# Norm of the b projection done tile by tile within the second half of gated output a, with the split of its key/value weights

## The reference, cut to what matters

```python
            h = h + (o * jax.nn.silu(gate)) @ w_out_a[i]
        else:
            if layer == N_A_LAYERS:
                u_kv = rmsnorm(h, kv_norm_g)
                k_s, v_s = jnp.split(u_kv @ w_kv, [KV_WIDTH_B], axis=-1)
...
            u = rmsnorm(h, norm_b_g[j])
            q, gate = jnp.split(u @ w_in_b[j], [WIDTH_B], axis=-1)
```

## Time and profile before

| | |
|---|---|
| median of 3 runs | 2799.35 us (2794.68 to 2800.64) |
| the profiled execution: its own time | 2794.62 us |
| its span, first to last instruction | 2792.8 us |
| TensorE busy with matmuls | 2515.3 us, 90% |
| VectorE busy | 1630.2 us, 58% |
| ScalarE busy | 1351.0 us, 48% |
| mean granted TensorE clock | 0.965 |

### The profile page before, as it was taken

How to read it: one execution, slowest core, us unless ns; L and a number is a source line. 1 busy time by engine, 2 the same in 40 slices (tenths; PEclk the granted TensorE clock), 3 DMA queues, 4 the chain that set the end, 5 groups by cost and what they waited for, 6 DMA issues and landing times. The chain is left out here.

```text
span 2792.8 us, 38108 instructions
## 1 busy us (share of the span) xinstructions
PE 2515.3 (90%) x13535; PEld 1999.3 (72%) x13547; DVE 1630.2 (58%) x2854; ACT 1351.0 (48%) x2357; POOL 401.7 (14%) x558
## 2 busy tenths in 40 slices
PE   1899699999975999999977999997999897998989
PEld 1687369888754888888865878885666676886667
DVE  5663645587646999999957145412555517651751
ACT  3253144597335788888856132323555404322850
POOL 0122012230201211111111000001222200000330
PEclk9999899999997999999998999998999998999999
DMA  6542000000228999999967111033010212113301
GB/s 231 162 140 79 0 0 1 1 1 32 90 92 342 403 412 410 411 414 414 418 248 270 51 42 62 23 136 128 31 62 17 103 54 86 31 38 118 117 12 50
DMA packets 126957, 400.27 MB, mean 143 GB/s; under 512 B 11975, under 2 KB 62284, under 8 KB 114398
## 3 DMA queue, kind: packets, MB, share of 16 engines
q1 hardware_dynamic: 113754, 354.07, 33.4%
q0 software_dynamic: 12048, 42.56, 3.9%
q10 hardware_dynamic: 1012, 1.72, 0.2%
HBM read 347.93 MB, written 50.40 MB: 143 GB/s over the span
## 5 line engine op out<-in xcount | busy, mean ns | idle before, releaser
L2736 DVE CUSTOM_DVE_ANT_0 fox_l<-PS,fox_c 128x256 f32<-128x256 f32 (+7 forms) x128 | 92.1, 756 | 129.7 <-PE PS L2783 83.2
L2673 ACT ACTIVATE fox_l<-fox_l,stat 128x256 f32<-128x256 f32 (+7 forms) x128 | 98.3, 769 | 80.6 <-DVE stat L2736 80.5
L329 PE MATMUL PS<-wehg,xsTh 128*128 128x512 f32 x256 | 100.4, 392 | 8.3 <-DVE we0g_rest L2152 6.9
L329 PE MATMUL PS<-wehd,aTh 128*128 128x512 f32 x256 | 100.7, 393 | 6.6 <-DVE aTl L2171 6.6
L329 PE MATMUL PS<-wqkh,uTh 128*128 128x512 f32 x256 | 103.1, 403 | 0.0
L329 PE MATMUL PS<-wehu,xsTh 128*128 128x512 f32 x256 | 102.9, 402 | 0.0
L331 PE MATMUL PS<-wqkh,uTl 128*128 128x512 f32 x256 | 100.5, 392 | 0.0
L331 PE MATMUL PS<-wehd,aTl 128*128 128x512 f32 x256 | 100.4, 392 | 0.0
L331 PE MATMUL PS<-wehg,xsTl 128*128 128x512 f32 x256 | 100.2, 392 | 0.0
L331 PE MATMUL PS<-wehu,xsTl 128*128 128x512 f32 x256 | 100.1, 391 | 0.0
L330 PE MATMUL PS<-wqk_rest,uTh 128*128 128x512 f32 x256 | 100.0, 391 | 0.0
(11 more groups left out here) (579 smaller groups left out, 7525.4 us busy)
## 6 DMA issues: line engine op xcount, KB each, us to landing
we0g<-in_w_expert_gate SPq DMA_DIRECT2D x16, 2048.0 KB
we0u<-in_w_expert_up SPq DMA_DIRECT2D x16, 2048.0 KB
we1g<-in_w_expert_gate SPq DMA_DIRECT2D x16, 2048.0 KB, 11.2
we0d<-in_w_expert_down SPq DMA_DIRECT2D x16, 2048.0 KB
we1u<-in_w_expert_up SPq DMA_DIRECT2D x16, 2048.0 KB
we1d<-in_w_expert_down SPq DMA_DIRECT2D x16, 2048.0 KB
wada_rest<-in_w_ada SPq DMA_DIRECT2D x16, 1024.0 KB, 5.5
wada<-in_w_ada SPq DMA_DIRECT2D x4, 2048.0 KB, 12.9
```

What stands on the lines that cost most here:

```text
L329: nc.tensor.matmul(out, lh, rh, start=start, stop=False)
L2673: nc.scalar.activation(prob(p, e)[:, 0:K], prob(p, e)[:, 0:K], ACT.Exp, bias=nbm[:, u % 8:u % 8 + 1], scale=-1.0, accum_out=rsum[:, u % 16 ...
L2736: nc.vector.tensor_tensor_reduce(out=prob(p, e)[:, 0:K], in0=PS[:, 2 * e:2 * e + 2, :].rearrange("p a b -> p (a b)")[:, 0:K], in1=C[:, h % ...
```

## The change

A new function, `phase_gated_out_norm`, takes the place of gated output a and of the norm block. Its first half is as before. In the second half, when a token tile's right 512 columns have been added, the tile is complete, and its norm follows at once: ScalarE squares it and takes the root, VectorE scales it, and TensorE transposes it (8 blocks of 128x128) behind the next unit's matmuls. The key/value weights are loaded at the end of the first half and split in the second, with the gain as the scale of ScalarE's copy and of one VectorE operation, in eight pieces of 128x512. Output units use PSUM banks 0 to 3 (before 0 to 7), transposes banks 4 to 7. The b projection starts with its matmuls. Tiles move to other slots to make room.

```diff
+def phase_gated_out_norm(nc, A, env, sem, O, wo, loads, hi_slots, H, h_in, h_load, h_store, extra):
...
+    xn = [m.at(f"xn_nb{j}", 11, [P, D], kib=4 * j) for j in range(2)]
...
+    KV_AT = {1: (0,), 2: (1,), 3: (2,), 4: (3,), 5: (4,), 6: (5, 6), 7: (7,)}
...
+    def bank(t, half):
+        return PS[:, 4 + 2 * (t % 2) + half, :]
...
+            for u in range(2 * T):
+                n, t = u // T, u % T
+                sp.wait_ge(h_done, u + 1)
+                if u == T - 1:
+
+                    sp.dma_start(kv[:, :, :], chunk_of(A["w_kv_2"], slice(0, HALF))).then_inc(env.wkv_in, 16)
+                sp.dma_start(h_store[t * P:(t + 1) * P, n * HALF:(n + 1) * HALF], H[:, t, n * HALF:(n + 1) * HALF]
+                             ).then_inc(saved, 16)
...
+        @block.scalar
+        def _(act):
+            def high(t):
+                for half in range(2):
+                    act.wait_ge(t_ready, 2 * t + half + 1)
+                    nc.scalar.activation(turned(xTh, t, half), bank(t, half).rearrange("p (a b) -> p a b", b=P),
+                                         ACT.Identity).then_inc(x_hi, 1)
...
+            extra["act"](act)
+            act.wait_ge(o_mm, T)
+            for t in range(T):
+                act.wait_ge(h_done, T + t + 1)
+                if t >= 2:
+                    act.wait_ge(t_ready, 2 * (t - 1))
+                nc.scalar.activation(xn[t % 2][:, :], H[:, t, :], ACT.Square, accum_out=ss[:, t:t + 1]
+                                     ).then_inc(squares, 1)
+                act.wait_ge(squares, t + 1)
+                nc.scalar.activation(rs[:, t:t + 1], ss[:, t:t + 1], ACT.Sqrt, bias=env.eps[:, 0:1], scale=1.0 / D
+                                     ).then_inc(rms, 1)
+                if t:
+                    high(t - 1)
+                for k in KV_AT.get(t, ()):
+                    act.wait_ge(env.wkv_in, 16)
+                    nc.scalar.activation(kvh[:, k, :], kv[:, k, :], ACT.Identity, scale=gain[:, k:k + 1]
+                                         ).then_inc(kv_hi, 1)
+            high(T - 1)
...
+            for u in range(2 * T):
+                n, t = u // T, u % T
+                h = slice(n * HALF, (n + 1) * HALF)
+                dve.wait_ge(o_mm, u + 1)
+                nc.vector.tensor_tensor(H[:, t, h], PS[:, u % 4, :], H[:, t, h], ALU.add).then_inc(h_done, 1)
+                if n == 0:
+                    continue
+                for k in KV_AT.get(t - 1, ()):
+                    dve.wait_ge(kv_hi, k + 1)
+                    nc.vector.scalar_tensor_tensor(kvl[:, k, :], kv[:, k, :], gain[:, k:k + 1],
+                                                   kvh[:, k, :].bitcast(F32), ALU.mult, ALU.subtract)
+                one = slice(t, t + 1)
+                dve.wait_ge(rms, t + 1)
+                do(nc.vector.reciprocal(rs[:, one], rs[:, one]))
...
+                nc.vector.tensor_scalar(xn[t % 2][:, :], H[:, t, :], rs[:, one], None, ALU.mult).then_inc(xn_ready, 1)
+                if t:
+                    rest(t - 1)
+            for k in KV_AT[T - 1]:
...
+            rest(T - 1)
...
+            def turn(t):
+                pe.wait_ge(xn_ready, t + 1)
+                if t >= 2:
+                    pe.wait_ge(x_lo, 2 * (t - 1))
+                for half in range(2):
+                    for c in range(4):
+                        k = 4 * half + c
+                        last = nc.tensor.transpose(bank(t, half)[:, c * P:(c + 1) * P],
+                                                   xn[t % 2][:, k * P:(k + 1) * P], env.ident)
+                    last.then_inc(t_ready, 1)
...
+                if u >= 4:
+                    pe.wait_ge(h_done, u - 3)
...
+                if n == 1 and t >= 1:
+                    turn(t - 1)
+            turn(T - 1)
...
-            for p in range(4):
-                group_hi(0, p)
...
-            group_gain(0, 0)
-            for p in range(1, 4):
-                group_gain(0, p)
-                group_lo(0, p - 1)
-            group_lo(0, 3)
...
-    phase_gated_out(nc, A, env, sem, "a", env.O_a, env.wo_a, env.wo_a[1:], (8, 10), H, sem("h_in_a"),
-                    env.h_dram, [env.ha_dram], extra=trig)
-    env.wkv, env.wkv_in = m.at("wkv", 9, [P, KD, HALF]), sem("wkv_in")
+    env.wkv, env.wkv_in = m.at("wkv", 7, [P, KD, HALF]), sem("wkv_in")
+    env.wkvh, env.wkvl = m.at("wkvh", 8, [P, KD, HALF], F32R), m.rest("wkv")
     env.xT = (m.at("xTh", 3, [P, KD, S], F32R), m.at("xTl", 5, [P, KD, S], F32R))
-    phase_norm(nc, env, sem, "nb", H, None, [], 10, m.at("junk_nb", 7, [P, 2, D]),
-               prefetch=[(env.wkv, env.wkv_in, chunk_of(A["w_kv_2"], slice(0, HALF)))],
-               split=env.xT + (None,))
+    phase_gated_out_norm(nc, A, env, sem, env.O_a, env.wo_a, env.wo_a[1:], (8, 10), H, sem("h_in_a"),
+                         env.h_dram, env.ha_dram, trig)
     phase_b_projection(nc, A, env, sem)
```

More of the change, by code:

```diff
@@ L2883, in _, with wpiece, turned, do @@
                 last.then_inc(o_mm, 1)
+def phase_gated_out_norm(nc, A, env, sem, O, wo, loads, hi_slots, H, h_in, h_load, h_store, extra):
+    m, PS = env.m, env.PS
+    (Oh, Ol), (xTh, xTl) = O, env.xT
+    wl = [m.rest(f"wo_a{n}") for n in range(2)]
+    woh = [m.at(f"woh_a{n}", hi_slots[n], [P, KD, HALF], F32R) for n in range(2)]
+    xn = [m.at(f"xn_nb{j}", 11, [P, D], kib=4 * j) for j in range(2)]
+    kv, kvh, kvl = env.wkv, env.wkvh, env.wkvl
+    gain = env.cols[:, ROWS["kv_norm_g_2"]:ROWS["kv_norm_g_2"] + KD]
+    ss, rs, nw = env.stat[:, 0:T], env.stat[:, T:2 * T], env.stat[:, 2 * T:3 * T]
+    saved, w_hi, w_lo, o_mm, h_done = (sem("saved_a"), sem("w_hi_a"), sem("w_lo_a"), sem("o_mm_a"), sem("h_done_a"))
+    squares, rms, xn_ready, t_ready = sem("squares_nb"), sem("rms_nb"), sem("xn_nb"), sem("xnT_nb")
+    x_hi, x_lo, dve_step, kv_hi = sem("x_hi_nb"), sem("x_lo_nb"), sem("rstd_nb"), sem("kv_hi")
+    raw = [x[0] for x in wo]
+    KV_AT = {1: (0,), 2: (1,), 3: (2,), 4: (3,), 5: (4,), 6: (5, 6), 7: (7,)}
+    def wpiece(x, j):
+        return x[j // 4][:, 2 * (j % 4):2 * (j % 4) + 2, :]
+    def turned(x, t, half):
+        return x[:, 4 * half:4 * half + 4, t * P:(t + 1) * P]
+    def bank(t, half):
+        return PS[:, 4 + 2 * (t % 2) + half, :]
+    with nc.Block() as block:
+        @block.sync
+        def _(sp):
+            load(sp, loads)
+            for t in range(T):
+                sp.dma_start(H[:, t, :], h_load[t * P:(t + 1) * P, :]).then_inc(h_in, 16)
+            for u in range(2 * T):
[5 more added lines that the diff above has]
+                             ).then_inc(saved, 16)
+            sp.wait_ge(saved, 16 * 2 * T)
+        @block.gpsimd
+        def _(pool):
+            extra["pool"](pool)
+        @block.scalar
[5 more added lines that the diff above has]
+                                         ACT.Identity).then_inc(x_hi, 1)
+            for j in range(8):
+                act.wait_ge(wo[j // 4][1], 16)
+                nc.scalar.copy(wpiece(woh, j), wpiece(raw, j)).then_inc(w_hi, 1)
+            extra["act"](act)
+            act.wait_ge(o_mm, T)
+            for t in range(T):
+                act.wait_ge(h_done, T + t + 1)
[13 more added lines that the diff above has]
+            high(T - 1)
+        @block.vector
+        def _(dve):
+            step = Steps(dve_step)
+            def do(instruction):
+                dve.wait_ge(dve_step, step.mark(instruction))
+            def rest(t):
+                for half in range(2):
+                    dve.wait_ge(x_hi, 2 * t + half + 1)
+                    nc.vector.tensor_tensor(turned(xTl, t, half), bank(t, half).rearrange("p (a b) -> p a b", b=P),
+                                            turned(xTh, t, half).bitcast(F32), ALU.subtract).then_inc(x_lo, 1)
+            for j in range(8):
+                dve.wait_ge(w_hi, j + 1)
+                nc.vector.tensor_tensor(wpiece(wl, j), wpiece(raw, j), wpiece(woh, j).bitcast(F32), ALU.subtract
+                                        ).then_inc(w_lo, 1)
+            extra["dve"](dve)
+            dve.wait_ge(h_in, 16 * T)
+            for u in range(2 * T):
[12 more added lines that the diff above has]
+                do(nc.vector.reciprocal(rs[:, one], rs[:, one]))
+                do(nc.vector.tensor_tensor(nw[:, one], rs[:, one], rs[:, one], ALU.mult))
+                do(nc.vector.scalar_tensor_tensor(nw[:, one], ss[:, one], EPS * D, nw[:, one], ALU.add, ALU.mult))
+                do(nc.vector.tensor_scalar(nw[:, one], nw[:, one], -0.5 / D, 1.5, ALU.mult, ALU.add))
+                do(nc.vector.tensor_tensor(rs[:, one], rs[:, one], nw[:, one], ALU.mult))
+                nc.vector.tensor_scalar(xn[t % 2][:, :], H[:, t, :], rs[:, one], None, ALU.mult).then_inc(xn_ready, 1)
+                if t:
+                    rest(t - 1)
+            for k in KV_AT[T - 1]:
+                dve.wait_ge(kv_hi, k + 1)
+                nc.vector.scalar_tensor_tensor(kvl[:, k, :], kv[:, k, :], gain[:, k:k + 1],
```

(29 more changed lines are left out.)

23 lines of the change are left out of this document (11 added, 12 removed).

## The result

The changed kernel takes **2774.86 us** (median of 4 runs, 2770.27 to 2776.55) against 2798.80 us before (4 runs, 2794.68 to 2800.64): ratio 0.9916 (below 1 is faster), 95% interval 0.9905 to 0.9928. The forecast was 2775.8 us. One execution of an experiment, the one with one more square per tile, took 5166 us, for no reason that is known; it is left out of that experiment's median. The profiled execution took 2770.27 us with a span of 2768.1, 24.7 less than the 2792.8 of the earlier trace rows.

The account below looks back on a forecast made before the run. TensorE, busy 90% of the span, bounds the kernel, so only its idle or slow stretches can pay. 27.5 - 5.6 - 0.1 + 0.6 = 22.4 us off the 2798.2 us mean gives 2775.8 us, range 2768 to 2784.

Parts of the forecast that it names:

- Taken away, 27.5 us: Gated output a's last matmul to the b projection's first: 35.66 us shrinks to a tail of 8.15, saving 27.5 us.
- Added, 5.6 us: Second half of gated output a: six groups of eight transposes on TensorE's path at 0.94 us each, 5.6 us.
- the first tile's wait, 0.1: First tile of the second half: with the table load in its chain, TensorE waits 0.1 us at most.
- Clock, 0.6: Start of the b projection: half clock again, for 4.1 us instead of 5.3, gaining 0.6 us.
- Rival 1: Tail before the b projection: the clock holds, 2.05 us more gained, 2773.7 us; chance 0.10.
- The sum: Whole kernel: 27.5 - 5.6 - 0.1 + 0.6 = 22.4 us faster.
- the forecast's upper gain: Whole kernel: a gain of 24.7 us if the clock is kept and transpose groups cost 0.8 us each.
- rival 3: Second half: waits at every group make the clock halve, 168 slow matmuls, 31 us more, 2806 us; chance 0.04.
- Edits priced at nothing: Four-bank PSUM ring, moved weight loads (`wkv`, `wq`), store order, new slots and the old split's removal: no cost or further gain.
- 2 us of slack: Second half: a tile's chain takes 4.4 us, TensorE returns to that tile 6.4 us later, leaving 2 us.
- rival 2: Second half: a tile's chain outlasts a unit; at 8 us, 13 us in all is lost, 2789 us; chance 0.10.
- the chain of 4.4 us: Each tile in the second half: from its unit's last matmul's start to its scaled tile, 4.4 us.

## Why the prediction was right, point by point

- **Taken away, 27.5 us.** Measured 35.66 - 7.76 = 27.9. The tail went as forecast, in its order and bound by VectorE's list: the last group started 4.44 us after the last output matmul (forecast 4.4), the last rest ended at +7.43 (forecast +7.8; the two rests take 1.28 together, not 1.38), the next stage began 0.33 later (0.3).
- **Added, 5.6 us, and the first tile's wait, 0.1.** The second and the eighth add of the half lie 2302.83 - 2264.57 = 38.3 us apart, six intervals with 5.44 of matmuls in each: 5.6 added. Of it 0.2 belong to the first tile (its interval is 6.53, the others 6.33 to 6.37; its group starts 0.34 us behind the unit's last matmul, the others 0.23, so the wait itself is 0.1) and 5.4 are six groups of 0.90 (forecast 0.94). The experiment with doubled groups showed that this is a price of the transposes themselves. In ScalarE's timeline the first tile's table load of 1.28 is followed by the root at once, as in the earlier trace rows:

```profile
2261.08 1.28 ACT L2954 ACT_TABLE_LOAD   x1
2262.38 0.29 ACT L2954 ACTIVATE stat<-stat,eps 128x1 f32<-128x1 f32 x1
```

  The further drain of the Trainium skill (ScalarE: Activation LUTs, What ACT_TABLE_LOAD costs) is not seen here either.
- **Clock, 0.6.** Half clock in b from its start at 2310.16 to within 2314 to 2315, about 4.3 us instead of 5.3; from b's first matmul to the first unit's copy are 8.1 us instead of 8.7, so 0.6. The value was right, but two of the experiments, in which the clock held, show that it could as well have been 2.6: here I was lucky. Rival 1 did not come, but its reasoning and that of the forecast fail alike: I took the 3.3 us of the earlier trace rows for the pause that the clock bears. The pauses were 3.17 and 2.12 us, both shorter, and it fell. The kernel before had already shown more: it was still at 1.00 in 2321 to 2322, 4 us after its first transposes had ended.
- **The sum.** 27.9 - 5.6 + 0.6 = 22.9 by these rows, less 0.4 in the stage's first half, where the half clock at the start lasted 4.3 us instead of 3.6 (the first half's last add starts 45.9 us after the first matmul, before 45.5): 22.5, as the stage has it; forecast 22.4. The rest of the profiled difference, 2.2, is elsewhere and moves from run to run. The mean of the runs before as a base met the median. Two slips in the sums around it: the forecast's upper gain, with the clock kept and groups at 0.8, adds up to 25.2 us, not 24.7, and rival 3's 168 x 0.18 is 30, not 31.
- **Edits priced at nothing.** Right: TensorE was busy 44.10 of 44.10 us with four output banks, and VectorE began on `wq` with no idle time.
- **What was wrong** is the step "2 us of slack", and with it rival 2's price. I compared the chain with TensorE's return to the tile and left out that VectorE's own list closes a shorter loop: the next add stands behind the rests. The slack was 1.2 us, and past it the excess is paid in full at each tile. With the 3.6 us of rival 2 that is, as an estimate, 3.5 at the first tile (which rival 2's sum left out), 2.4 at six intervals and 3.6 in the tail, some 21 us instead of 13. The forecast did not need it, since the chain of 4.4 us was right.
- **Rival 3** needed waits, and there are none: clock 1.00 through the second half. Where an experiment made waits, the clock did swing between 1.00 and 0.50, as the rule of the Trainium skill has it (TensorE: Matmul & The Clock Gate, A second HAM failure mode: psum-queue depth-cycling). The ring of four banks and the transposes between the units are in the changed kernel too, which stayed at 1.00, so they alone do not make it swing; whether they have a part in it once there are waits, no run tells.

## What to carry to other kernels

A small stage between two stages of matmuls is worth its whole length, less what of it must stay on TensorE: price the moved transposes at full, and everything on the other engines at nothing as long as each tile's list fits in a tile's time. For that fit, follow each engine's own list round the loop from one tile's first instruction to the next tile's; the idle time before that instruction is the slack (here 1.2 us), not the distance to the consumer's return (2.2 us). And what is left at the end is the last tile's chain: fill it with a piece of the next stage that needs only earlier tiles.

## What the runs showed of the hardware

The granted clock after a pause of TensorE is not settled by the length of that pause. In the kernel with four more squares two pauses of 2.87 and 2.85 us, each behind a unit of matmuls at clock 1.00, ended one at 1.00 and one at 0.50. It fell in tails with pauses of 3.17 and then 2.12 us with 1.2 us of transposes between (in the changed kernel within 2307 to 2308, during the transposes), and held with 2.29 and 1.84 us and 1.97 us of transposes; with 3.17 us ahead of doubled transposes it fell during them. Nor is the time from the end of work to the fall fixed: it was 3.3 us in the earlier trace rows and 2.0 us in the first wait of the kernel with four more squares. From b's first matmul to the first unit's copy (the kernel with that unit in the tail left aside) it took 6.0 us where the clock held and 7.4 to 8.7 us where it had fallen, so each case is worth 1.4 to 2.7 us, up to as much as a whole part of the change.
